# A mixture-of-experts layer on one Trainium2 core: the expert weights walked in two stretches of 1792 columns instead of four of 896

## The reference

```python
def swiglu(x, wg, wu, wd):
    return (jax.nn.silu(x @ wg) * (x @ wu)) @ wd

def moe_swiglu(x, w_router, we_gate, we_up, we_down):
    ...
    for e in range(N_EXPERTS):
        out = out + combine[..., e:e + 1] * swiglu(x, we_gate[e], we_up[e], we_down[e])
    return out
```

## Time and profile before

| | us |
|---|---|
| median of 3 runs | 1293.39 |
| lowest, highest | 1290.77, 1293.57 |
| the profiled execution: its time | 1285.44 |
| the profiled execution: span from the first to the last instruction | 1283.7 |

### The profile page before, as it was taken

How to read it: one execution, slowest core, us unless ns; L and a number is a source line. 1 busy time by engine, 2 the same in 40 slices (tenths; PEclk the granted TensorE clock), 3 DMA queues, 4 the chain that set the end, 5 groups by cost and what they waited for, 6 DMA issues and landing times.

```text
span 1283.7 us, 15887 instructions
## 1 busy us (share of the span) xinstructions
PE 1225.5 (95%) x6199; PEld 1056.5 (82%) x6199; DVE 1110.8 (87%) x871; ACT 936.2 (73%) x720; POOL 55.4 (4%) x57
## 2 busy tenths in 40 slices
PE   9999999999999999999999998999999999999875
PEld 8988888888988888888787887878788788887654
DVE  6978555568879999998999998999999999999897
ACT  5575444454858787888878888888888778888773
POOL 0100000001010000000000010000000000000130
PEclk9999999999999999999999999999999999999998
DMA  9948655537458999999999999999999999999992
GB/s 319 344 159 262 197 184 184 191 123 247 164 178 331 373 409 397 401 413 410 410 404 406 399 410 413 409 395 409 411 411 411 410 403 411 409 412 403 411 413 96
DMA packets 143557, 434.49 MB, mean 338 GB/s; under 512 B 8965, under 2 KB 50997, under 8 KB 131189
## 3 DMA queue, kind: packets, MB, share of 16 engines
q1 hardware_dynamic: 139936, 421.07, 85.4%
q0 software_dynamic: 3456, 12.32, 2.8%
q10 hardware_dynamic: 84, 0.02, 0.0%
HBM read 428.40 MB, written 4.98 MB: 338 GB/s over the span
## 4 chain that ended last, share of the span: by engine, by line
PE 61%; DVE 17%; DMA 15%; ACT 5%; issue 3%; SPq 0%; DVEq 0%; ACTq 0%
DVE w_lo L1022 14%; PE turn L1686 6%; PE turn L1688 6%; PE turn L1687 6%; DMA raw<-in_we_down 6%; PE accp L1686 6%; PE accp L1688 5%; PE accp L1687 5%; PE turn L1798 4%; PE turn L1795 4%; DMA raw<-in_we_gate 4%; DMA raw<-in_we_up 4%; ACT w_hi L657 3%; PE turn L1797 2%; PE turn L1796 2%
## 5 line engine op out<-in xcount | busy, mean ns | idle before, releaser
L1022 DVE TENSOR_TENSOR w_lo<-raw,w_hi 128x1792 fp32r<-128x1792 f32 (+3 forms) x449 | 899.2, 2039 | 97.7 <-ACT w_hi L657 94.5
L657 ACT CAST w_hi<-raw 128x1792 fp32r<-128x1792 f32 (+2 forms) x443 | 759.5, 1726 | 173.3 <-PE turn L1688 46.7
L2112 PE MATMUL turn<-w_hi,t_both 128*128 128x448 f32 x512 | 192.6, 376 | 16.2 <-DVE w_lo L1022 15.6
L2113 PE MATMUL turn<-w_lo,t_both 128*128 128x448 f32 x512 | 187.9, 367 | 0.0
L1686 PE MATMUL turn<-w_hi,a_hi 128*128 128x448 f32 x496 | 184.1, 371 | 1.5 <-DVE w_lo L1022 1.5
L1688 PE MATMUL turn<-w_hi,a_lo 128*128 128x448 f32 x496 | 181.7, 366 | 0.0
L1687 PE MATMUL turn<-w_lo,a_hi 128*128 128x448 f32 x496 | 181.6, 366 | 0.0
L2112 PEld LDWEIGHTS turn<-w_hi,t_both 128*128 128x128 f32 x512 | 96.8, 189 | 35.3 <-issue 18.6
L2113 PEld LDWEIGHTS turn<-w_lo,t_both 128*128 128x128 f32 x512 | 96.9, 189 | 7.8
L1686 PEld LDWEIGHTS turn<-w_hi,a_hi 128*128 128x128 f32 x496 | 93.1, 188 | 11.5 <-DVE w_lo L1022 1.9
L1687 PEld LDWEIGHTS turn<-w_lo,a_hi 128*128 128x128 f32 x496 | 93.2, 188 | 8.4
(11 more groups left out here) (291 smaller groups left out, 1525.2 us busy)
## 6 DMA issues: line engine op xcount, KB each, us to landing
raw<-in_we_gate SPq DMA_DIRECT2D x128, 896.0 KB, 8.5
raw<-in_we_up SPq DMA_DIRECT2D x128, 896.0 KB, 9.1
raw<-in_we_down SPq DMA_DIRECT2D x96, 1024.0 KB, 9.6
raw<-in_w_in SPq DMA_DIRECT2D x18, 1024.0 KB, 8.8
raw<-in_we_down SPq DMA_DIRECT2D x32, 512.0 KB, 8.5
raw<-in_w_down SPq DMA_DIRECT2D x11, 1024.0 KB, 5.0
raw<-in_w_gate SPq DMA_DIRECT2D x10, 1024.0 KB, 5.2
raw<-in_w_up SPq DMA_DIRECT2D x10, 1024.0 KB, 5.2
```

The source lines that it names most:

```text
L657: nc.scalar.copy(w_hi[:, p % PARTS, 0:filled(p)], raw[:, p % RING, 0:filled(p)]).then_inc(hi_done, 1)
L1022: return nc.vector.tensor_tensor(out, whole, hi.bitcast(f32), ALU.subtract)
L2112: nc.tensor.matmul(to[:, c, :], few, wh[:, kk, c, :], start=(k == 0), stop=False)
L2113: last = nc.tensor.matmul(to[:, c, :], few, wl[:, kk, c, :], start=False, stop=(k == KD - 1))
```

## The change

An expert is walked in two stretches of 1792 columns instead of four quarters, so there are 16 units. A gate or up piece is now one block of 128 rows by 1792 columns: 896 KB as before, in runs of 7 KB. A unit has 8 gate pieces, 8 up pieces and 7 down pieces, all down pieces of 256 rows (1 MB): 23 pieces where two quarters had 24. The sums of gate take all four banks of `turn`; up then takes the same four banks, and the transposed product the same again. So that PE has something to do at each change, three down pieces of the unit before stand between gate and up, and four between up and the next gate. SiLU, multiplication, transposes and the split of the product are each done in two halves. SiLU is written into `h_e` and multiplied there. Unit 0 has its up sums in `accp`, so the ranking key is read out of there earlier (`key_known`). `first_gate` has three passes for the first four pieces only. The last expert's last down pieces go through `last_down` for the last eight of 14 blocks. The positions of the other work (`VISITS`, `SUM_AT`, `add_rows`) are moved.

```diff
--- before.py
+++ after.py
...
-    QUARTERS = 4
-    WIDE = FF_E // QUARTERS
-    PART = WIDE // 2
+    STRETCHES = 2
+    WIDE = FF_E // STRETCHES
+    PART = WIDE // 4
     BLOCKS = WIDE // P
-    N_UNITS = E * QUARTERS
-    U_PIECES = 12
+    D_PIECES = BLOCKS // 2
+    N_UNITS = E * STRETCHES
+    U_PIECES = 2 * KD + D_PIECES
...
-    ORDER = "HHH" + "LH" * 12 + "H" + "L" * QUARTERS
-    assert ORDER.count("H") == HEAVIES * QUARTERS and ORDER.count("L") == LIGHTS * QUARTERS
+    ORDER = "HH" + "LH" * 6 + "L" * STRETCHES
...
-    VISITS = ((2, 0), (3, 1), (8, 2), (10, 3), (13, 4), (16, 5), (20, 6))
+    VISITS = ((1, 0), (2, 1), (3, 2), (5, 3), (7, 4), (9, 5), (11, 6))
...
-    SUM_AT = (1, 4, 5, 6)
-    PICK_AT = 7
+    SUM_AT = (0, 1, 3, 7)
+    PICK_AT = 13
...
-        return "uuuu" if i == 0 else "uuuudddd" if i == N_UNITS - 1 else "uduududd" if light(i) else "uduuuddd"
-
...
-        which, _, pair = IN_ORDER[p - MOE_AT]
-        return len(blocks_of(pair)) * D if which == "down" else 2 * WIDE
+        return PIECE if IN_ORDER[p - MOE_AT][0] == "down" else WIDE
...
+        H_PARTS = ((0, 6), (6, BLOCKS))
+
+        def two_banks(of, half):
+            return of[:, 2 * half:2 * half + 2, 0:PART]
+
+        def two_parts(a, half):
+            return a[:, 2 * half * PART:2 * (half + 1) * PART].rearrange("p (c f) -> p c f", c=2)
+
+        def up_banks(i):
+            return turn if i else accp
+
+        def hT_bank(i, part):
+            b0, b1 = H_PARTS[part]
+            to = up_banks(i)[:, 2 * part:2 * part + 2, :].rearrange("p b c -> p (b c)")
+            n = FEW if light(i) else P
+            return to[:, 0:(b1 - b0) * n].rearrange("p (b t) -> p b t", t=n)
...
-                    load(PLACE[which, i, pair],
-                         expert_rows(w, ORDER[i], k)[:, 2 * pair:2 * pair + 2, s * WIDE:(s + 1) * WIDE])
+                    load(PLACE[which, i, j], expert_rows(w, ORDER[i], k)[:, j:j + 1, s * WIDE:(s + 1) * WIDE])
...
+                used(gate_piece(i, KD - 1))
+                for half in range(2):
+                    if light(i):
+                        if number(i) > 1:
+                            act.wait_ge(few_added, 4 * (number(i) - 1))
+                        nc.scalar.copy(two_parts(few_low, half), two_banks(turn, half)).then_inc(few_kept, 1)
+                    else:
+                        nc.scalar.activation(two_parts(h_e, half), two_banks(turn, half), ACT.Silu).then_inc(e_silu, 1)
...
+                g7, u7 = gate_piece(i, KD - 1), up_piece(i, KD - 1)
+                if kept_at(i) is not None:
+                    splits_to(gate_piece(i, 2))
+                    keep_ys(kept_at(i))
+                splits_to(g7 + 2)
+                leave_gate(i)
+                if i in (1, 2):
+                    scale_tokens(i - 1)
+                if light(i):
+                    splits_to(g7 + (4 if visit_at(i) is None else 3))
+                    silu_few(i)
+                splits_to(g7 + 4)
                 if visit_at(i) is not None:
                     round_tokens(visit_at(i))
                 if i == PICK_AT:
                     copy_pick()
...
+                splits_to(u7 + 2)
                 if light(i):
                     leave_up(i)
...
+                splits_to(u7 + (5 if light(i) else 4))
+                round_h(i, 0)
+                splits_to(u7 + (6 if light(i) else 5))
+                round_h(i, 1)
+            splits_to(MOE_AT + MOE_PIECES - 1)
...
+            def times_up(i, half):
+                dve.wait_ge(e_silu, 2 * i + half + 1)
+                rows = slice(0, FEW if light(i) else P)
                 if light(i):
...
+                    dve.wait_ge(few_added, 4 * (number(i) - 1) + 2 + half + 1)
                 else:
...
+                    used(up_piece(i, KD - 1))
+                h = two_parts(h_e[rows], half)
+                nc.vector.tensor_tensor(h, two_banks(up_banks(i)[rows], half), h, ALU.mult).then_inc(e_h, 1)
+
+            def rest_of_h(i, part):
+                b0, b1 = H_PARTS[part]
+                dve.wait_ge(e_hT_hi, 2 * i + part + 1)
                 if light(i):
...
+                    packed = hT_packed(i)[:, b0:b1, :]
+                    hi, lo = packed[:, :, 0:FEW], packed[:, :, FEW:P]
                 else:
...
+                    hi, lo = (a[:, b0 * P:b1 * P].rearrange("p (b t) -> p b t", t=P) for a in hT_pair(i))
+                rest_of(lo, hT_bank(i, part), hi).then_inc(e_hT_lo, 1)
...
+                g7, u7 = gate_piece(i, KD - 1), up_piece(i, KD - 1)
+                if i == 0:
+                    splits_to(g7)
+                    rank_experts()
                 if kept_at(i) is not None and KEPT[kept_at(i)][0] == "L":
+                    splits_to(gate_piece(i, 3))
                     fold_ys(kept_at(i))
...
+                splits_to(g7 + 4)
+                if i == 0:
+                    splits_to(up_piece(0, 6))
                 if i in SUM_AT:
                     know_tokens(SUM_AT.index(i))
...
                 if visit_at(i) is not None:
                     rest_of_tokens(visit_at(i))
...
+                if i < N_UNITS - 1:
+                    splits_to(up_piece(i, 4))
+                    amid_up(i)
+                else:
+                    for j, k in enumerate((2, 3, 6, 7)):
+                        splits_to(up_piece(i, k))
+                        add_rows(j)
+                splits_to(u7 + 3)
+                for half in range(2):
+                    times_up(i, half)
+                splits_to(u7 + 4)
+                rest_of_h(i, 0)
+                splits_to(u7 + 5)
+                rest_of_h(i, 1)
+            splits_to(MOE_AT + MOE_PIECES - 1)
...
+            def rows_piece(i, which, k):
+
+                e, _ = expert_step(i)
+                to = up_banks(i) if which else turn
+                w = split((up_piece if which else gate_piece)(i, k))
+                for c in range(4):
+                    if which and i and k == 0 and c % 2 == 0:
+                        pe.wait_ge(e_silu, 2 * i + c // 2 + 1)
+                    wh, wl = columns_of(w, c)
+                    if light(i):
+                        few = xg_few[e % 2][:, k, :]
+                        nc.tensor.matmul(to[:, c, 0:PART], few, wh, start=(k == 0), stop=False)
+                        last = nc.tensor.matmul(to[:, c, 0:PART], few, wl, start=False, stop=(k == KD - 1))
+                    else:
+                        last = product(to[:, c, 0:PART], (xg_hi[e % 2][:, k, :], xg_lo[e % 2][:, k, :]), (wh, wl),
+                                       k == 0, k == KD - 1)
...
             def before_gate(i):
 
-                if visit_at(i - 1) is not None:
-                    pe.wait_ge(xg_done, visit_at(i - 1) + 1)
-                if i - 1 in SUM_AT:
-                    pe.wait_ge(tokens_known, SUM_AT.index(i - 1) + 1)
-                if i - 1 == PICK_AT:
+                if i == 1:
+                    pe.wait_ge(e_silu, 2)
+                    pe.wait_ge(tokens_known, 1)
+                else:
+                    pe.wait_ge(e_hT_lo, 2 * i)
+
+            def before_up(i):
+
+                if i == 0:
+                    pe.wait_ge(key_known, 1)
+                elif i in SUM_AT:
+                    pe.wait_ge(tokens_known, SUM_AT.index(i) + 1)
+                if visit_at(i) is not None:
+                    pe.wait_ge(xg_done, visit_at(i) + 1)
+                if i == PICK_AT:
                     pe.wait_ge(slots_read, 1)
 
-            def amid_up(i):
-
-                gate_left(i)
+            def between(i):
+
+                pe.wait_ge(e_silu, 2 * i + 2)
...
+                pe.wait_ge(xg_hi_ready, 2)
+                for k in range(4):
+                    pe.wait_ge(hi_done, MOE_AT + k - 1)
+                    for c in range(4):
+                        nc.tensor.matmul(turn[:, c, 0:PART], xg_hi[0][:, k, :], columns_of(w[k], c)[0],
                                          start=(k == 0), stop=False)
...
+                pe.wait_ge(xg_lo_ready, 1)
+                for k in range(4):
+                    pe.wait_ge(*split_of(MOE_AT + k))
+                    for c in range(4):
+                        wh, wl = columns_of(w[k], c)
+                        nc.tensor.matmul(turn[:, c, 0:PART], xg_hi[0][:, k, :], wl, start=False, stop=False)
+                        last = nc.tensor.matmul(turn[:, c, 0:PART], xg_lo[0][:, k, :], wh, start=False, stop=False)
+                    last.then_inc(piece_used, 1)
+                pe.wait_ge(xg_lo_ready, 2)
+                for k in range(4, KD):
+                    rows_piece(0, 0, k)
...
+                    for k in range(KD):
+                        rows_piece(i, 0, k)
+                        if i == 1 and k < 2:
+                            turn_h(0, k)
+                    down(i - 1, 0)
+                    if light(i):
+                        add_low(i, 0)
                     else:
```

(30 more changed lines are left out.)

331 lines of the change are left out of this document (99 added, 232 removed).

## The result

The changed kernel takes **1317.13 us** (median of 4 runs, 1314.10 to 1319.90) where the kernel before takes 1292.44 beside it (1290.77 to 1293.57): ratio 1.0192, 95% interval 1.0164 to 1.0219. It is 25 us slower; forecast were 12 us less. Its profiled execution took 1316.03 us, span 1314.2.

What follows compares the result with a forecast made beforehand. DMA was taken as the bound, by 2 us over PE in heavy units and 4 to 5 over DVE. Terms -18.0 + 3 + 1.9 + 1 = -12.1 us took the median 1293.4 to 1281.3 us, range 1271 to 1296.

Steps and rivals of the forecast that it cites:

- the part on the banks: Waits from gate, up and the next gate using the same PE banks: +3 us over 16 units, bounds nothing to 24.
- Gate to up in a heavy unit: At a heavy unit's change from gate to up, SiLU is done before PE needs the banks: nothing.
- Packets: Gate, up and down transfers: 34,816 fewer packets, 2,176 per engine at 8.3 ns each: -18.0 us.
- The 7.7 ns from two of the stretches: Packet cost beside its bytes, from a line through the gate-and-up-only stretch and a second stretch of transfers.
- The ring: Piece slots at up to next gate: two slots, 4.6 us, spare against DVE's 3.5 us lateness; +3 us in all.
- The ring runs dry at each swap: Rival at unit ends: DVE's lump and PE's wait coincide, DMA stands 1.5 us each; 1299 us, chance 0.14.
- up to the next gate, VectorE's lump: Unit's end: DVE does product halves and splits in 8.4 us while 4.9 us of pieces land, 3.5 us late.
- VectorE as the bound: Rival over the whole layer: DVE's ceiling is 94% busy, so time stays at 1292 us; chance 0.08.
- The first units: Start, where PE leads: +3.4 us of PE over DMA, less earlier freeing in first_gate; together +1.9 us (0 to +5).
- The end: Last 25 us, set by DVE, adding steps waiting for fetched rows as the risk: +1 us (-1 to +7.4).
- The 8 us from the profiled execution to the median: Whole kernel: the profiled execution lies 8 us under the runs' median; difference carried, so 1273.3 became 1281.3 us.

Runs made afterwards that it cites:

- e3: Changed kernel with ScalarE rounding down's third piece before the SiLU in heavy units: 1302.72 us, r 1.0091.
- e1: Kernel before with gate and up read in runs of 7 KB (other columns, so not the layer's output): 1280.62 us, r 0.9919.
- e2: Changed kernel with gate and up read in runs of 3.5 KB again (other columns): 1323.06 us, r 1.0261.
- mended: The changed kernel with the edits of e3 and e5, that is the kernel of e5: 1299.56 us, r 1.0066.
- e13: Mended kernel with gate and up read in runs of 3.5 KB again (other columns): 1304.00 us, r 1.0108.
- e7: Changed kernel with five ring slots in place of six: 1348.00 us, r 1.0426.
- e8: Kernel before with five ring slots in place of six: 1311.39 us, r 1.0186.
- e10: On e3, VectorE's product made for half the columns of each half: 1293.32 us, r 1.0010.
- e11: Kernel before with each of VectorE's 32 products made on half the columns: 1281.80 us, r 0.9922.
- e17: On e5, the lo part of up's sixth piece made for half its columns in 15 units: 1298.61 us, r 1.0054.
- e9: On e5, the heavy units' two transposes, with hi and lo of h, one down piece later each: 1300.67 us, r 1.0060.
- e5: On e3, the last two of VectorE's four adding steps moved behind down's pieces of the end: 1299.56 us, r 1.0066.
- e12: On e5, VectorE's two products of a unit put one split apart: 1301.23 us, r 1.0071.
- e18: Mended kernel with two matmuls for each three in heavy gate and up (low times high left out): 1294.84 us, r 1.0025.
- e14: On e5, GpSimd makes the lo part of one piece in each of 15 units: 1324.46 us, r 1.0261.
- e15: Kernel before with GpSimd making the lo part of 13 pieces: 1293.30 us, r 1.0011.
- e16: Kernel before with GpSimd making the lo part of 27 pieces: 1293.56 us, r 1.0024.
- e6: Kernel before with two matmuls for each three in heavy gate and up (low times high left out): 1286.48 us, r 0.9951.

## Why the prediction was wrong

**The step that failed** is in the part on the banks: "Gate to up in a heavy unit: [...] so SiLU is there first: nothing." It asked only whether the SiLU would be there when PE needs it, paced PE by the landings (down pieces "each landing 2.6 us after the other"), and took ScalarE to have time; what stands behind the SiLU in ScalarE's program was put at nothing. The trace of the changed kernel shows the reverse: at the end of a heavy gate PE is behind by all its split places, ScalarE has nothing to do but wait for it, and its program has the SiLU ahead of a split. The same text had the sum for it: "PE needs 2.43 us per gate or up piece where 2.2 us of DMA bring one, 1.8 us behind after eight", but used it for the ring and not for who waits for gate's last matmul. Undone by one digit (e3), it measured **14.4 us** (13 by the ratios) of the 24.7. In the kernel before the same instruction waited 6.5 us in all.

**Packets**, forecast at -18.0. In the kernel before the rows alone gave -11.7 (e1), 5.7 ns each and not 8.3, or 7.0 ns by the trace up to the first adding step; in the changed kernel 6 to 9 us (e2), mended 4 to 5 (e13). So this term was too large as well: by its price, and since the changed kernel is not bound by its transfers throughout. A transfer's price counts as far as transfers are the last to come; the more the engines stand, the less. The Trainium skill's "fixed ~3-cycle overhead per packet" ("DMA: Bandwidth & Descriptors", section "Why small descriptors are slow (HBM only)"), 3.5 ns at the page's 850 MHz, makes an estimated 7.2 us of e1's 2,048 packets. That is below the measured 11.7, though inside its interval (6.7 to 14.2 by the ratio), and half of the trace's 14.4. The 7.7 ns from two of the stretches come nearest to the trace's 7.0.

**The ring**, forecast at +3 with "two slots, 4.6 us, are spare". Windows at a share of 0.87 to 0.94 show no slot spare there, and a slot less costs 31 us (e7), in the kernel before 18 to 24 (e8). The rival "The ring runs dry at each swap" was the right kind, with 1299 us. Its place (up to the next gate, VectorE's lump) is the smaller part: the deep dips stand at heavy gates' ends. But it is a part: half of each product gives 8.5 us up to the first adding step in the changed order and 1.1 in the kernel before (e10, e11).

**VectorE as the bound.** The rival gave it a ceiling of 94% over the whole layer, and the sum set it 4 to 5 us per stretch under the transfers. The changed order shows neither: 15 us of its work are worth 9.4 us at the products and 1 us elsewhere (e10, e17), so where it stands decides, not how much there is. What the products have and a split has not is the chain behind them: product, transposes, hi, lo, and in the mended kernel the gate that needs their banks (e9).

**The first units**, forecast at +1.9: no run took them apart. From 380 to 480 us the changed kernel moved 361 GB/s and the one before 369, so 0.8 MB less or an estimated 2 us, two of the eight stands of the SiLU among them. **The end**, forecast at +1 with 7.4 as the bound: VectorE stood 2.36 and 3.04 us for the two last fetches, and e5 gave back 3.2.

**The 8 us from the profiled execution to the median** were carried over to the changed kernel as they were. They belong to the last fetch of the kernel before, as far as the traces tell (1.07 us of stand at 1285.44 us, 8.5 in the slower ones), and the changed kernel moved that fetch: its profiled execution lies 1.1 us under its median. Trace against trace the change cost 30.6 us, where the sum had 12.1 less, so the miss of the order of work is larger than the medians show.

**What stays open.** The mended kernel is still 7 us over the kernel before by the medians and 12.7 by the traces (1298.16 against 1285.44), with 4 to 5 us won from packets in it. VectorE's idle time from 380 us on is 916.4 - 836.5 = 79.9 us in it, against 66.1. Moving TensorE's transposes (e9), parting the two products (e12) and halving splits amid up (e17) each gave nothing or 1 us; less TensorE work (e18) gave 5. That the work at the units' ends is on the path there and was not before is shown (e10 against e11, by one trace each). That it gets there through the shared banks is argued, not shown: no kernel gave the mended order banks of its own, since gate at 1792 columns fills four and the sums have the rest. No version with all the work in it beats the kernel before. e1 shows what the kernel before would win by longer runs, but it reads other columns; a layout of the weights that has two quarters' columns side by side would be needed.

## What to carry to other kernels

Where an engine works in program order behind small rings, a new wait costs not its own time but that of all that is queued behind it: for each wait that a change adds or moves, ask which engine is late at that moment (the waits name it, and "[0.73 <-PE]" in front of every split is the sign), and put whatever doesn't depend on the late one ahead. Price a saving on transfers by an edit that changes it alone, in the kernel at hand; the same 32,768 packets were worth 11.7, 6 to 9 and 4 to 5 us in three versions of the kernel. Test a cut of work in two places before calling an engine the bound. And before a gain in one kernel is set beside a gain in another, look at a mark in the middle of both traces: e10 and e11 gained the same by their medians, and for different reasons.

## What the runs showed of the hardware

With runs of 7 KB the rate reached 423 GB/s at a share of 1.01 (window 720 to 740 us above), where no slice of the kernel before is over 413. GpSimd took 4.5 us for the lo part of a piece that VectorE makes in 2.03 (e14), and VectorE's longest split was 4.55 us in e14, 4.19 in e15 and 4.12 in e16, against 2.30 without this edit. One indirect fetch of rows, in the same place, landed after 16.3 us in the trace of the kernel before and after 23.6 to 23.7 in those of e1, e6 and e15.
